# One block for the feed-forward part of a layer: routing, experts and embedding without a barrier between them, token weights computed behind the first row fetch, the embedding input projected in the expert tail, and shared value tiles

## The reference, cut to what matters

```python
h = h + hierarchical_moe(rms_norm(h, ffn_norm[i]), w_router_group[i], b_router_group[i],
                         w_router_expert[i], b_router_expert[i], w1[i], w3[i], w2[i])
h = h + per_layer_embedding(h, p[i], ple_norm[i], w_ple_gate[i], w_ple_proj[i])
```

## Time and profile before

| what | value |
|---|---|
| three runs | 2092.26, 2094.64, 2095.2 us (median 2094.64) |
| profiled execution, its own time | 2092.71 us |
| its span in the profile | 2090.9 us |
| TensorE busy | 1896.9 us (91%) |
| VectorE, ScalarE, GpSimd busy | 753.3, 503.7, 104.4 us |
| 192 loads of expert weights, 2 MB each | median 26.2 us from issue to landing |
| DMA in the expert stages | 1.01 of 16 engines, 421 GB/s |

### The profile page before, as it was taken

How to read it: one execution, slowest core, us unless ns; L and a number is a source line. 1 busy time by engine, 2 the same in 40 slices (tenths; PEclk the granted TensorE clock), 3 DMA queues, 4 the chain that set the end, 5 groups by cost and what they waited for, 6 DMA issues and landing times. The chain is left out here.

```text
span 2090.9 us, 22829 instructions
## 1 busy us (share of the span) xinstructions
PE 1896.9 (91%) x8452; PEld 937.7 (45%) x8452; DVE 753.3 (36%) x1449; ACT 503.7 (24%) x785; POOL 104.4 (5%) x84
## 2 busy tenths in 40 slices
PE   7899999999699999999979899979599999999978
PEld 5565555666433333333334475466433333333333
DVE  2444444442423433343331111164424333343331
ACT  3233333332111111111130423542111111111130
POOL 0111111110000000000000000000000000000000
PEclk8999999999799999999989999989799999999999
DMA  6111111020589999999971212111299999999931
GB/s 226 41 40 41 41 41 40 0 81 1 206 346 420 421 422 421 421 421 421 421 290 40 81 41 88 40 41 41 104 378 421 421 421 421 421 422 422 421 118 41
DMA packets 77071, 478.11 MB, mean 229 GB/s; under 512 B 6352, under 2 KB 6736, under 8 KB 26576
## 3 DMA queue, kind: packets, MB, share of 16 engines
q1 hardware_dynamic: 72400, 460.46, 53.9%
q0 software_dynamic: 4608, 16.78, 2.0%
HBM read 470.93 MB, written 6.29 MB: 228 GB/s over the span
## 5 line engine op out<-in xcount | busy, mean ns | idle before, releaser
L1322 PE MATMUL bank<-ring,xT 128*64 128x512 f32 x2048 | 467.6, 602 | 48.4 <-DMA ring<-in_w 47.3
L1322 PEld LDWEIGHTS bank<-ring,xT 128*64 128x64 f32 x2048 | 138.5, 137 | 327.1 <-issue 238.3
L1296 DVE TENSOR_TENSOR H<-H,bank 128x512 f32<-128x512 f32 x256 | 171.1, 688 | 261.0 <-PE bank L1309 260.5
L375 PE MATMUL bank<-ring,ring 128*128 128x512 f32 x512 | 250.4, 601 | 8.9 <-ACT ring L682 8.9
L1346 PE MATMUL bank<-ring,hT 128*64 128x512 f32 x1024 | 226.8, 596 | 0.5 <-ACT hT L1362 0.5
L1309 PE MATMUL bank<-yp,Sb 128*128 128x512 bf16 x768 | 189.4, 383 | 6.9 <-issue 6.4
L1309 PEld LDWEIGHTS bank<-yp,Sb 128*128 128x128 bf16 x768 | 67.4, 98 | 147.0 <-issue 83.3
L1346 PEld LDWEIGHTS bank<-ring,hT 128*64 128x64 f32 x1024 | 70.7, 137 | 133.0 <-issue 128.0
L843 PE MATMUL bank<-ring,ring 128*128 128x512 f32 x288 | 126.4, 593 | 0.2
L1283 DVE TENSOR_TENSOR y<-y,yp 128x512 f32<-128x512 f32 x64 | 44.3, 692 | 197.1 <-ACT yp L1371 197.1
L375 PEld LDWEIGHTS bank<-ring,ring 128*128 128x128 f32 x512 | 86.4, 193 | 59.7 <-issue 49.5
(11 more groups left out here) (237 smaller groups left out, 2070.8 us busy)
## 6 DMA issues: line engine op xcount, KB each, us to landing
ring<-in_w SPq DMA_DIRECT2D x192, 2048.0 KB, 26.2
ring<-in_w_heads SPq DMA_DIRECT2D x8, 2048.0 KB, 8.2
ring<-in_w_ple_gate SPq DMA_DIRECT2D x4, 2048.0 KB, 31.3
ring<-in_w_kv SPq DMA_DIRECT2D x3, 2048.0 KB, 14.7
ring<-in_b_w_q SPq DMA_DIRECT2D x3, 2048.0 KB, 8.2
ring<-in_a_w_out SPq DMA_DIRECT2D x2, 2048.0 KB, 13.9
rows<-ring SPq DMA_DIRECT2D x8, 512.0 KB, 10.6
H<-in_x SPq DMA_DIRECT2D x4, 512.0 KB, 4.9
```

The lines of the kernel that those rows point to most:

```text
L375: m = pe.matmul(bank[j % 2][:, :], w[:, c, j, :], k.xnT[:, c, :], start=(c == 0), stop=(c == DC - 1))
L1296: dve.tensor_tensor(out, out, k.bank[6 + j % 2][:, :], ALU.add).then_inc(s.added, 1)
L1322: last = pe.matmul(out[e * SLOTS:(e + 1) * SLOTS, :], k.xT[:, at, e * SLOTS:(e + 1) * SLOTS], w[:, e, c, :], start=(at == 0), stop=(at == ...
```

## The change

The four blocks of a layer become one (`feed_forward`), with one barrier at its end. Each block's code becomes a function per engine, and the streams simply follow each other. Besides that:

- VectorE computes the ranks first. The count for `more_experts` (`count_passes`) and the tokens' weights (`weigh_tokens`) follow after the first pair's row fetch has been released. `identify` is split in two, since slots are known before weights. The first pair starts its products when half of its transposed rows are there, and pair 1's slots are identified after its first two quarters.
- The last pair's results are spread tile by tile through banks 0 to 3 (`spread_last`, `add_last`), so that a tile of `H` is final after two additions. The sums of squares of tiles 0 to 2 are taken by ScalarE as they become final, that of tile 3 by VectorE.
- `from_p(0)` and `(1)` stand ahead of the last spread, `(2)` and `(3)` behind it. `pT` and `w_proj` are loaded ahead of the gate's halves, and `w_kv` behind them without a barrier.
- The value products of groups 1 and 2 share one tile of 512 columns.

```diff
-def prefetch_ple(sp, k, layer):
-
+def load_ple(k, layer, load):
+
+    load(2, k.R.flat(2, 2048), k.w_proj[layer].rearrange("(p c) n -> p (c n)", c=2))
...
+    def units(self):
+
+        return [(0, d) for d in range(NT)] + [(1, d) for d in range(NT)]
+
     def tensor(self, pe, s):
         k = self.k
-        for g in range(GROUPS):
-            w = k.R.flat(3 + g).rearrange("p (c n) -> p c n", c=DC)[:, :, KVPG * HD:]
-            for d in range(NT):
-                n = g * NT + d
-                if n >= 2:
-                    pe.wait_ge(s.v, n - 1)
-                for c in range(DC):
-                    x = k.xnT[:, c, d * P:(d + 1) * P] if g == 0 else k.xnT[:, c, d::4]
-                    last = pe.matmul(k.bank[6 + n % 2][:, 0:KVPG * HD], x, w[:, c, :], start=(c == 0),
+        w = k.ring[:, 3:3 + GROUPS, :].rearrange("p g (c n) -> p g c n", c=DC)[:, :, :, KVPG * HD:]
+        for n, (strided, d) in enumerate(self.units()):
+            if n >= 2:
+                pe.wait_ge(s.v, n - 1)
+            for c in range(DC):
+                if strided:
+                    last = pe.matmul(k.bank[6 + n % 2][:, :], k.xnT[:, c, d::4], w[:, 1:, c, :], start=(c == 0),
                                      stop=(c == DC - 1))
-                last.then_inc(s.vproj, 1)
+                else:
+                    last = pe.matmul(k.bank[6 + n % 2][:, 0:KVPG * HD], k.xnT[:, c, d * P:(d + 1) * P], w[:, 0, c, :],
+                                     start=(c == 0), stop=(c == DC - 1))
...
+def weigh_tokens(dve, k, s):
...
+def count_passes(dve, k, s, layer):
+
+    ch = s.chain
+    total = k.bank[1][:, NT * EXPERTS:(NT + 1) * EXPERTS]
+    dve.tensor_reduce(k.most[:, :], total, AX.X, ALU.max).then_inc(s.most, 1)
+    dve.wait_ge(s.most, 1)
+    ch.link(dve.tensor_scalar(k.most_i[:, :], k.most[:, :], 1.0, None, ALU.subtract))
+    dve.tensor_scalar(k.extra[:, layer:layer + 1], k.most_i[:, :], SLOTS.bit_length() - 1,
+                      None, ALU.logical_shift_right).then_inc(s.extra, 1)
...
+def add_last(dve, k, s, i):
+
+    for m in range(2 * NT):
+        t, n = m // 2, m % 2
+        dve.wait_ge(s.spread, 8 * i + m + 1)
+        out = k.H[:, t, n * HALF:(n + 1) * HALF]
+        dve.tensor_tensor(out, out, k.bank[m % 4][:, :], ALU.add).then_inc(s.added, 1)
+
+
+def spread_last(pe, k, s, i):
+
+    pe.wait_ge(s.Sb, i + 1)
+    for m in range(2 * NT):
+        t, n = m // 2, m % 2
+        if m < 2:
+            pe.wait_ge(s.low, 2 * i + n + 1)
+        if m >= 4:
+            pe.wait_ge(s.added, 8 * i + m - 3)
+        for q, part in enumerate(halves_of(k, n)[1]):
+            last = pe.matmul(k.bank[m % 4][:, :], k.Sb[:, t * P:(t + 1) * P], part, start=(q == 0), stop=(q == 2))
+        last.then_inc(s.spread, 1)
...
+        if not (last or first):
+            identify_tokens(pe, k, s, i + 1, i + 1)
+            identify_weights(pe, k, s, i + 1, i + 1)
+        pe.wait_ge(s.xT, 2 * i + 1)
+        expert_up(pe, k, 0, 0, odd, k.bank[0], s.half0, arrived)
+        pe.wait_ge(s.xT, 2 * i + 2)
+        expert_up(pe, k, 0, 1, odd, k.bank[0], s.h1, arrived)
+        if first:
+            identify_tokens(pe, k, s, i + 1, i + 1)
+            identify_weights(pe, k, s, i + 1, i + 1)
+        if first:
+            pe.wait_ge(r.extra, 1)
...
+    pe.wait_ge(r.places, 1)
+    identify_tokens(pe, k, s, 0, 0)
+    pe.wait_ge(r.parts, 1)
+    identify_weights(pe, k, s, 0, 0)
+    turn_rows(pe, k, s, 0, 0)
+    turn_rows(pe, k, s, 0, 1)
...
+    build_slots(dve, k, s, 0, 0)
+    place_slots(dve, k, s, 0, 0)
+    count_passes(dve, k, r, layer)
+    weigh_tokens(dve, k, r)
+    weigh_slots(dve, k, s, 0, 0)
+    evacuate_rows(dve, k, s, layer, 0, 0)
+    evacuate_rows(dve, k, s, layer, 0, 1)
+    build_slots(dve, k, s, 1, 1)
+    dve.wait_ge(r.tokens, 16)
+    pair(0, first=True)
...
+    sp.wait_ge(r.logits, 1)
+    sp.wait_ge(s.xg, 16)
+    load_expert_pair(k, layer, 1, load_of(1, True), odd=True)
...
+def more_experts(eng, k, s, r, layer, body, first=None, then=None):
+
+    eng.wait_ge(r.extra, 1)
+    extra = eng.value_load(k.extra[0:1, layer:layer + 1], min_val=0, max_val=SEQ // SLOTS - 1)
+    with eng.If(extra > 0):
+        if first:
+            first()
+        with eng.Fori(0, extra) as p:
+            with eng.Fori(0, PAIRS) as pair:
+                i = p * PAIRS + pair
+                eng.wait_ge(s.done, i + 1)
+                body(i, pair)
+        if then:
+            eng.wait_ge(s.done, extra * PAIRS + 1)
+            then()
...
+def from_p(pe, k, j):
+
+    n, t = j // NT, j % NT
+    w = k.R.flat(2, 2048).rearrange("p (c n) -> p c n", c=2)
+    for c in range(2):
+        last = pe.matmul(k.bank[4 + j % 4][:, :], k.pT[:, c, t * P:(t + 1) * P],
+                         w[:, c, n * HALF:(n + 1) * HALF], start=(c == 0), stop=(c == 1))
+    return last
+
+
+def embed_tensor(pe, k, s):
+
+    R = k.R
+    norm_tensor(pe, k, s, chunks=range(4), banks=4)
+    norm_tensor(pe, k, s, chunks=range(4, DC), banks=4)
+    norm_chunk(pe, s, DC - 2)
+    norm_chunk(pe, s, DC - 1)
...
+    settled = [(s.added, 8 * (PAIRS - 1) + 2 * (t + 1)) for t in range(NT)]
+    by_scalar, by_vector = (0, 1, 2), (3,)
...
+            route_tensor(pe, k, r, layer)
+            experts_tensor(pe, k, s, r, layer)
+            s.gates_landed = [(k.R.landed[n], (k.R.takes[n] + 1) * 16) for n in range(2)]
+            k.R.arrived(pe, 2)
+            pe.wait_ge(e.p, 16)
+            from_p(pe, k, 0)
+            from_p(pe, k, 1)
+            spread_last(pe, k, s, PAIRS - 1)
+            pe.wait_ge(s.added, 8 * (PAIRS - 1))
+            from_p(pe, k, 2)
+            from_p(pe, k, 3).then_inc(e.early, 1)
+
+            def again():
+                pe.wait_ge(m.reloaded, 16 * 3)
+                for j in range(4):
+                    from_p(pe, k, j)
+
+            more_experts(pe, k, m, r, layer, lambda i, pair: more_tensor(pe, k, m, i, pair), then=again)
+            embed_tensor(pe, k, e)
...
+            route_vector(dve, k, r, layer)
+            experts_vector(dve, k, s, r, layer)
+            dve.wait_ge(s.added, 8 * PAIRS)
+            dve.sem_inc(m.done, 1)
+            more_experts(dve, k, m, r, layer, lambda i, pair: more_vector(dve, k, m, layer, i, pair))
+            norm_vector_rows(dve, k, e, settled, by_vector)
+            embed_vector(dve, k, e, layer)
...
             load_sqrt_table(act, k)
+            norm_scalar_rows(act, k, e, settled, by_scalar)
+            embed_scalar(act, k, e, layer)
...
+            def ple(slot, dst, src):
+                sp.wait_ge(s.frees[slot], PAIRS if slot == 2 else PAIRS - 1)
+                sp.dma_start(dst, src).then_inc(k.R.landed[slot], 16)
...
+            store_rows(sp, k, r, layer)
+            experts_loads(sp, k, s, r, layer)
+            sp.dma_start(k.pT[:, :, :], k.p_t[layer].rearrange("(p c) n -> p c n", c=2)).then_inc(e.p, 16)
+            load_ple(k, layer, ple)
...
-                route(k, layer)
-                experts(k, layer, lambda sp: prefetch_ple(sp, k, layer))
-                more_experts(k, layer, lambda sp: prefetch_ple(sp, k, layer))
-            end_phase()
-            with phase():
                 k.sg = sb("sg", [P, 2, HALF])
                 k.pT = sb("pT", [P, 2, SEQ])
-                embed(k, layer, load_kv if layer == 0 else (lambda sp: None), store=(layer == 1))
+                feed_forward(k, layer, load_kv if layer == 0 else None)
```

More of the change, by code:

```diff
@@ L1192, in build_slots, with identify_tokens @@
     dve.tensor_scalar(ranks, ranks, float(SLOTS), None, ALU.subtract).then_inc(s.shift, 1)
-def identify(pe, k, s, pair, i, alone=False):
+def identify_tokens(pe, k, s, pair, i, alone=False):
     pe.wait_ge(s.slots, i + 1)
@@ new lines, in more_tensor @@
+def more_tensor(pe, k, s, i, pair):
+    identify_tokens(pe, k, s, pair, i, alone=True)
+    identify_weights(pe, k, s, pair, i)
+    turn_rows(pe, k, s, i, 0)
+    turn_rows(pe, k, s, i, 1)
+    pe.wait_ge(s.landed, (i + 1) * (16 * RING))
+    pe.wait_ge(s.xT, 2 * i + 2)
+    expert_up(pe, k, 0, 0, False, k.bank[0], s.half0, None)
+    expert_up(pe, k, 0, 1, False, k.bank[0], s.h1, None)
+    expert_up(pe, k, 1, 0, False, k.bank[1], s.half2, None)
+    expert_up(pe, k, 1, 1, False, k.bank[1], s.h3, None)
+    expert_turn(pe, k, s, i)
+    expert_down(pe, k, s, i, None, alone=True)
+    spread(pe, k, s, i, range(NT), alone=True)
+    spread(pe, k, s, i, range(NT, 2 * NT), alone=True)
@@ new lines, in more_vector @@
+def more_vector(dve, k, s, layer, i, pair):
+    build_slots(dve, k, s, pair, i, alone=True)
+    place_slots(dve, k, s, pair, i, alone=True)
+    weigh_slots(dve, k, s, pair, i)
+    evacuate_rows(dve, k, s, layer, i, 0)
+    evacuate_rows(dve, k, s, layer, i, 1)
+    mark_tokens(dve, k, s, pair, i, alone=True)
+    hidden(dve, k, s, i)
+    split_results(dve, k, s, i)
+    add_results(dve, k, s, i, range(2 * NT))
+    dve.wait_ge(s.shift, i + 1)
+    dve.wait_ge(s.added, 8 * i + 8)
+    dve.sem_inc(s.done, 1)
```

(31 more changed lines are left out.)

615 lines of the change are left out of this document (265 added, 350 removed).

## The result

The changed kernel takes 2060.16 us (median of four runs, 2057.83 to 2061.88) against 2094.57 us: a ratio of 0.9837, interval 0.9824 to 0.9850, so 34 us or 1.6% faster. The forecast was 2064.5 us in a range of 2059 to 2073.

The account below looks back on a forecast made before the run. The weight stream on full DMA engines (421 GB/s) bounds the expert stages, engine alternation the seams. Gains of 7.3 + 0.6 + 10 + 9 + 2.2 = 29.1 off 2092.71 give 2063.6, adjusted to 2064.5 us; range 2059 to 2073.

Parts of the forecast that it names:

- whatever starts the stream earlier moves the whole stage: Expert stage: weight stream sets the pace, so issuing pair 1's first load earlier, at the stage's head, moves the stage.
- the stream's end does not follow its start: Rival, 0.08: slots freed by PE, not the first load, set the pace; the head's 7.9 is lost, 2072 us.
- Head of a stage: Routing: ranks computed first let POOL's first row fetch start earlier; gain 3.65 us a layer, 7.3 in both.
- Pair 0: Stage's first pair: products start at half of the rows, removing 0.88 us of idle; 0.3 us a layer, 0.6 in all.
- The late rows: Rival, 0.15: pair 1's rows, asked for later, come late and hold PE 3.1 us in each layer; 2070.7 us.
- Tail, layer 0: Last down to gate in layer 0: gate starts at 1083.3 instead of 1094.28; gain 10 us.
- it spreads until 1067.3, does `from_p(2)` and `(3)` until 1070.7, reads the count, and branches: PE in layer 0's tail: branch of 3.80 us follows the products; with 0.9 around it, done at 1075.4.
- Tail, layer 1: Same steps in layer 1 with the short branch: 2014.3 instead of 2023.35, gain 9 us.
- Values: Value products: four units at 27.5 us replace eight at 29.9, a copy 0.3 longer; gain 2.2 us, between 0 and 2.4.
- `w_proj` lands with the gates: Rival, 0.07: transfers share engines, `w_proj` is in only by 1068, the last spread is held 10 us a layer; 2083 us.
- The long branch: Rival, 0.18: branch over the loop costs 3.8 us in layer 1 too, or twice that in layer 0; 2068 us.
- The slower rival: Rival, 0.03: longer block moves PE's loop code so each turn pays an instruction fetch; at 8 us a turn, 2104 us.

Follow-up runs that it names:

- early_load: The changed kernel with pair 1's first two loads no longer waiting for pair 0's rows; 2061.85 us, ratio 0.9845.
- pair0_whole: The changed kernel with pair 0 in one piece, pair 1 identified ahead of its first product, as before; 2063.81 us, ratio 0.9852.
- its control: The changed kernel itself, unaltered, run again on the chip of the later experiments; 2060.11 us, ratio 0.9831.
- p_behind_branch: The changed kernel with products 2 and 3 of the embedding input behind PE's branch over the loop instead of ahead of it; 2068.32 us, ratio 0.9869.
- early_read_kv: The changed kernel with the count read earlier on VectorE and PE, and loads held by a wait on the variance; 2060.12 us, ratio 0.9831.
- gates_first: The changed kernel with the gate's two halves loaded ahead of `w_proj`, as before; 2085.59 us, ratio 0.9959.

## Why the prediction was right, and where it was off

*What bounds the stage*: right. The 421 GB/s and the stage's length stayed. But the step "whatever starts the stream earlier moves the whole stage" named the wrong starter. `early_load` started it 14 us sooner for nothing. The second starter that the text names, PE's progress in pair 0, is the one that `early_load` leaves. `pair0_whole` agrees with it, within a scatter as large as its effect. The head's gain held because the same fetch releases PE and the first load; the rival "the stream's end does not follow its start" was true in its mechanism and wrong in its price.

*Head of a stage*, 3.65 a layer: measured 3.59. The weights ended 1.8 us before the rows landed.

*Pair 0*, 0.3 a layer: mis-sized. The first product came 1.24 earlier, since the second `xT` copy and pair 1's identification no longer stand ahead of the first product, and not only the 0.88 us of idle. How much of it reached the stage's end is not shown: from the rows' landing to the last down's end it is 479.9 and 480.4 us before, 480.1 and 479.4 in the changed kernel, 479.0 and 479.5 in its control. The late rows did not come: the fetch of 590.00 landed at 594.5, in 4.54 us, in time for 595.71.

*Tail, layer 0*, 10: measured 14.3, the largest error. From the last down to the gate the sum had 25.6 us, and it was 21.3. The step that failed is "it spreads until 1067.3, does `from_p(2)` and `(3)` until 1070.7, reads the count, and branches". The reading and the branch belong to the sequencer, and they began at 1065.4 and 1066.3, before those products ran. A longer branch (6.27) so ended 14.2 us behind the last down, and the transpositions began at 14.3, where the sum had 16.7 with 3.80. This is 2.4 of the 4.3. `p_behind_branch` shows the cover: moved behind the branch, the same products cost 5.7 us. The other 1.9 were charges for a slow clock (7.9 for transpositions that took 7.0, and 1.0 for the products).

The rule of the Trainium skill that the prediction names ("Runtime: NRT & Kernel Launch", section "Instruction fetch mechanics") agrees with a branch that takes 0.33 us at one place and 3.8 to 6.7 at another. No run shows which code PE held at either. That the length also depends on data loads in flight is what `early_read_kv` adds.

*Tail, layer 1*, 9: measured 10.15. The transpositions start at the first normalised rows, 1.46 us after the variance, and not after the last as the sum had it. They then take longer for it.

*Values*, 2.2, where the prediction's own terms give 2.1 (29.9 - 27.5 - 0.3): 2.2 between the traces over a stretch that scatters by 2 us and more; alone 2.5 by the medians and 1.4 by the trace. Its size is not known better than that.

*The gate's weights in layer 0*, nothing: right. Their halves landed at 1063.5 and 1068.9 (1063 and 1068.5 in the forecast) and were needed at 1079.7.

*The rivals.* "`w_proj` lands with the gates" did not come, since it is ahead of them in the queue; `gates_first` shows that it would have cost 12.6 and 13.1 us, where I had 10. The long branch came in layer 0, with 6.27 us where the prediction calls more than 4 a sign of being wrong. It cost 0.3 us, since it ran beside issued products. The slower rival did not come: in the loop over pairs PE is busy for 237.5 us of 260, against 239.4, at the same GB/s.

*The sum*: 4.9 + 4.9 in the heads, 14.3 + 10.15 in the tails and 2.2 for the values are 36.5. Given back were 1.4 and 0.3 in the stages and 0.7 behind the last gate, the cause of which is open. 34.1 remain, as the medians have it (34.4). The two profiled executions differ by only 30.9, since in that of the changed kernel the first 80 us took 3.1 longer. Both kernels are alike up to there, and over the traces of this study the counts came anywhere from 567.6 to 572.2. The forecast's 29.1 was short in both tails and in pair 0; the result lies in the range, but only 1.2 us above its lower end.

## What to carry to other kernels

A wait that a block end hides is found by the distance between the last useful instruction and the next, engine by engine; most of this change's gain was there and not in the stage itself, 478 us long. Put work of PE's array ahead of a branch and not behind it: the sequencer takes the branch while the array still works. It matters where the branch is long (layer 0), and made no difference where it took 0.34 us. When several things start together, undo their tie one by one before calling one of them the cause.
